# Order of the four query blocks within a group of two attention loops: narrow, wide, middle narrow, middle wide

## The reference, cut to what matters

```python
# first loop: nsa_attention, the selected and the window branch
s = jnp.einsum('bgmqd,bgqkld->bgmqkl', qb, ks)           # selected keys
o_sel = jnp.einsum('bgmqkl,bgqkld->bgmqd', softmax(s, tok <= tq), vs)
s = jnp.einsum('bgmqd,bgsd->bgmqs', qb, kwb)             # window keys
o_win = jnp.einsum('bgmqs,bgsd->bgmqd', masked_softmax(s, win_ok), vwb)

# second loop: dilated attention (8 heads) and forgetting attention (8 heads)
s = jnp.einsum('bqhd,bkhd->bhqk', qi, k) * SCALE          # + bias or decay
s = jnp.where(k_pos[None, :] <= q_pos[:, None], s, NEG_INF_2)
o = jnp.einsum('bhqk,bkhd->bqhd', jax.nn.softmax(s, axis=-1), v)
```

## Time and profile before

| | us |
|---|---|
| median of 3 runs (1836.47 to 1839.16) | 1838.65 |
| span of the profiled execution | 1837.4 |
| first loop in it, first scores to the end | 98.2 |
| second loop in it, first scores to the end | 82.0 |

### The profile page before, as it was taken

The page is one execution under the profiler, slowest core; times in us unless marked ns, Lnnn a source line. Parts: engine busy times, 40 slices in busy tenths (PEclk is TensorE's granted clock), DMA queues, the critical chain, the costliest instruction groups (busy, mean ns, idle before and its releaser), DMA issues. The chain is left out here.

```text
span 1837.4 us, 22565 instructions
## 1 busy us (share of the span) xinstructions
PE 1760.4 (96%) x9024; PEld 1289.9 (70%) x9024; DVE 858.7 (47%) x1672; ACT 627.8 (34%) x1248; POOL 235.1 (13%) x286
## 2 busy tenths in 40 slices
PE   7999999999999999999999999999999989999993
PEld 6778888888888787568888888888766663333330
DVE  4436544543367345745554453263347562333224
ACT  5236344323353224635433332253347320000001
POOL 4000000000001003310000000000014404333322
PEclk9999999999999998999999999999999999999997
DMA  7223333332232217303333322332320158999974
GB/s 236 90 76 84 100 91 91 97 109 92 92 121 92 69 65 228 111 25 91 92 95 109 93 92 92 104 127 91 93 92 24 55 228 330 376 398 389 380 311 151
DMA packets 179528, 261.02 MB, mean 142 GB/s; under 512 B 18904, under 2 KB 134824, under 8 KB 167152
## 3 DMA queue, kind: packets, MB, share of 16 engines
q1 hardware_dynamic: 155824, 204.66, 33.2%
q0 software_dynamic: 19584, 25.77, 4.4%
q10 hardware_dynamic: 4032, 29.36, 4.1%
HBM read 297.53 MB, written 29.40 MB: 178 GB/s over the span
## 5 line engine op out<-in xcount | busy, mean ns | idle before, releaser
L189 PE MATMUL PB<-RING_R,OPS_R 128*128 128x512 f32 (+1 forms) x1056 | 414.7, 393 | 5.1 <-DVE RING_R L152 4.1
L191 PE MATMUL PB<-RING_R,OPS_R 128*128 128x512 f32 (+1 forms) x1056 | 409.1, 387 | 0.0
L190 PE MATMUL PB<-RING_R,OPS_R 128*128 128x512 f32 (+1 forms) x1056 | 408.9, 387 | 0.0
L169 DVE SCALAR_TENSOR_TENSOR RING_R<-RING,gains,RING_R 128x256 fp32r<-128x256 f32 (+2 forms) x456 | 219.4, 551 | 253.8 <-ACT RING_R L167 253.8
L189 PE MATMUL PB<-OPS_R,RING_R 128*128 128x512 f32 (+1 forms) x736 | 280.7, 381 | 0.0
L190 PE MATMUL PB<-OPS_R,RING_R 128*128 128x512 f32 (+1 forms) x736 | 279.5, 380 | 0.0
L191 PE MATMUL PB<-OPS_R,RING_R 128*128 128x512 f32 (+1 forms) x736 | 279.5, 380 | 0.0
L189 PEld LDWEIGHTS PB<-RING_R,OPS_R 128*128 128x128 f32 x1056 | 198.8, 188 | 48.4 <-DVE RING_R L152 5.3
L167 ACT ACTIVATE RING_R<-RING,gains 128x256 fp32r<-128x256 f32 (+2 forms) x456 | 209.9, 541 | 59.2 <-DMA RING<-in_w_in 47.7
L191 PEld LDWEIGHTS PB<-RING_R,OPS_R 128*128 128x128 f32 x1056 | 198.8, 188 | 40.7
L190 PEld LDWEIGHTS PB<-RING_R,OPS_R 128*128 128x128 f32 x1056 | 199.0, 188 | 38.9 <-issue 0.2
(11 more groups left out here) (379 smaller groups left out, 2033.1 us busy)
## 6 DMA issues: line engine op xcount, KB each, us to landing
RING<-in_ffn_w_gate SPq DMA_DIRECT2D x44, 512.0 KB, 4.0
RING<-in_ffn_w_up SPq DMA_DIRECT2D x44, 512.0 KB, 5.2
RING<-in_ffn_w_down SPq DMA_DIRECT2D x44, 512.0 KB, 4.2
RING<-in_w_expert_gate SPq DMA_DIRECT2D x16, 1024.0 KB, 8.0
RING<-in_w_expert_up SPq DMA_DIRECT2D x16, 1024.0 KB, 11.6
OPS<-in_w_expert_gate SPq DMA_DIRECT2D x16, 1024.0 KB, 13.6
OPS<-in_w_expert_up SPq DMA_DIRECT2D x16, 1024.0 KB, 16.2
Y<-in_w_expert_down ACTq DMA_DIRECT2D x14, 1024.0 KB, 9.6
```

Source lines behind the costliest of these rows:

```text
L169: t = nc.vector.scalar_tensor_tensor(by_k(RING_R, o)[:, :, k, :], raw, g, high.bitcast(fp32), ALU.mult, ALU.subtract)
L189: nc.tensor.matmul(o, x[0], w[0], start=start, stop=False)
L190: nc.tensor.matmul(o, x[0], w[1], start=False, stop=False)
L191: return nc.tensor.matmul(o, x[1], w[0], start=False, stop=stop)
```

## The change

The units are the same; the list order differs. In the first loop the branch r is now outside the block i, so that both runs over the four blocks follow one another; in both loops the blocks come in the order 0, 3, 1, 2, in widths w1 w4 w2 w3. Two conditions in values() of the second loop, which stood for "first unit of a group" and "last unit of a group", are rewritten so that they still mean that. All waits on semaphores count units, not widths, and the counts are made by functions that go by the width of each unit, so they follow.

```diff
@@ -1511,7 +1511,8 @@
-        NSA = [(c, i, r) for c in range(4) for i in range(MT) for r in range(2)]
+        BY_WIDTH = (0, 3, 1, 2)
+        NSA = [(c, i, r) for c in range(4) for r in range(2) for i in BY_WIDTH]
@@ -1913,7 +1914,7 @@
-        TWO = [(f, c, i) for f in range(2) for c in range(4) for i in range(MT)]
+        TWO = [(f, c, i) for f in range(2) for c in range(4) for i in BY_WIDTH]
@@ -1995,7 +1996,7 @@
-                if i == 0 and n >= 2:
+                if u % MT == 0 and n >= 2:
@@ -2007,7 +2008,7 @@
-                if i == MT - 1:
+                if u % MT == MT - 1:
```

## The result

The kernel with the new order takes 1842.3 us (median of 20 runs, 1837.8 to 1850.7), the kernel before on the same chips 1838.6 (20 runs, 1836.5 to 1843.1). The ratio is 1.0022, 95% interval 1.0013 to 1.0031: slower by 3.7 us. The forecast was 1838.3 and no change. The profiled execution has a span of 1839.9 us, before 1837.4.

The account below looks back on a forecast made before the run. It took chains through several engines to bound the two loops, PE being busy 96% of the span. First loop -0.4 and second +0.1 made -0.3 us, so 1838.65 became 1838.3, no change; range 1834.3 to 1842.5.

Parts of the forecast that it names:

- sum of distances: Both loops: times between successive values steps on PE, added per group; 9.28 us for the new order against 9.41.
- the paragraph on PE's clock: Low level only from 711.5 to 725.5, costing 0.40 us per us; upper level for the rest of the first loop.
- turn 15 is a w3: First loop: DVE's maxima and 2.3 us split precede the w3 copy; 4.2 instead of 2.24, so 2.0 us more.
- With the release where it is: Assumes the first loop's 14 us low-clock stretch ends as before, leaving the forecast sum at -0.3 us.
- the clock stays low longer: Rival, first loop's start: release 14 us later costs 5.6 us, giving 1843.9; chance 4%.
- A clock row below 1.00 behind 730: Sign in the first loop's clock that would prove the rival of a longer low clock, 1843.9 us.
- The clock rises sooner: Rival, first loop's start: a shorter low stretch saves 4 us, giving 1834.3; chance 7%.
- DVE late for the wide copies: Rival, both loops: late maxima delay the w3 copy, 16 x 0.33 = 5.3 us, giving 1843.6; chance 8%.
- Scores hidden: Rival: every distance a copy chain, a group 8.62 instead of 9.28, 10.6 us less, 1827.7; chance 4%.
- scores chain: Distance set by PE's values, transposes and scores in order; for w2 behind w4 2.69 us, against copy chain 2.31.

Follow-up runs that it names:

- e1: Changed kernel with the new order in the first loop alone, the second loop keeping rising width; 1841.9 us, ratio 1.0015 to the kernel before.
- e6: Changed kernel with no weight split inside the first loop, both chunks split behind it; 1840.5 us, ratio 1.0002 to the kernel before.
- e3: Changed kernel with the first loop's weight splits one turn later (ACT in turns 15, 23; DVE in 16, 24); 1831.0 us, ratio 0.9955 to the kernel before.
- e5: Kernel before (old order) with the first loop's weight splits one turn later; 1839.0 us, ratio 1.0001 to the kernel before.
- e9: Changed kernel with DVE's part of each first-loop split in halves, in turns 16 and 18 (24 and 26); 1831.3 us, ratio 0.9958 to the kernel before.
- e4: Kernel before (old order) with two unread DVE reductions behind each first-loop weight split; 1843.7 us, ratio 1.0026 to the kernel before.
- e10: New order with splits one turn later, plus two unread DVE reductions ahead of the w3 copies of turns 15 and 23; 1840.0 us, ratio 1.0007 to the kernel before.
- e7: Changed kernel with DVE's part of each first-loop split in halves, in turns 15 and 17 (23 and 25); 1834.8 us, ratio 0.9976 to the kernel before.

## Why the prediction was wrong

**The sum of distances was right.** The first loop by its four groups, from the values of turns 7, 15, 23 and 31, in us:

| first loop | before | after | moved | forecast | same list, upper level |
|---|---|---|---|---|---|
| first scores to turn 7 | 32.01 | 29.17 | -2.8 | -0.4 | |
| to turn 15 | 22.94 | 23.47 | +0.5 | +0.6 | |
| to turn 23 | 21.94 | 26.73 | +4.8 | +0.7 | +0.6 (e1, 22.52) |
| to turn 31 | 20.25 | 21.97 | +1.7 | -1.1 | -1.0 (e6, 19.26, no split) |
| last values | 1.02 | 0.80 | -0.2 | -0.2 | |

Where the clock is up, each group is within about 0.1 us of the forecast. The second loop confirms it: a group with f = 0 is 9.29 (forecast 9.28), with f = 1 9.71 (1401.05 to 1410.76; forecast 9.74), the two with sums and split 21.45 (21.7), the fourth values 12.4 behind the first scores (12.6). In all it moved by -0.3, forecast +0.1.

**The step that failed is the paragraph on PE's clock.** It read the earlier trace rows rightly, one low stretch at the start, and then treated its release as all that could move: everything behind it was taken at the upper level, "for the rest". The same text had worked out the cause of the new falls: "turn 15 is a w3 ... 4.2 instead of 2.24". It priced that as 2.0 us of wait and went on. It had the earlier trace rows beside it, a fall right behind a wait of 1.23, and didn't ask whether a wait of 2.2 that the change makes could do the same. It does: behind 757 and 784 the profile has 10.2 + 6.8 = 17.1 us of low clock, and by 0.4 each they are 6.8 us, which is the +4.2 and the +2.7 by which the third and fourth group exceed the same list at the upper level.

The same paragraph was wrong a second time, the other way: "With the release where it is" the first stretch was left at its 14 us, and it became 6.8. The first group moved by -2.8 where -0.4 was forecast, a figure given without its working.

Two of the rivals also leaned on the wait of the earlier trace rows staying as it was ("the same wait of PE stands in the same place", "PE's wait for ACT stays"). It doesn't: with the new list PE waits 0.60 in place of 1.23 us there, and the clock falls all the same (at 709.56), as PE's timeline of after shows:

```profile
705.50 3.76 PE L1619 MATMUL PB<-kcT,ST 64*128 64x32 f32 x64
709.87 1.23 PE L1555 MATMUL PB<-STG,ST 64*128 64x256 f32 x4 [0.60 <-ACT Z L1652]
```

All twelve profiles have a fall at this place, between 708.8 and 712.1, behind the third branch's 64 small matmuls. So the length of the wait alone doesn't decide; the work before it may count too, which no run separates.

**The rival that came nearest** was "the clock stays low longer". It had the kind, the price and its sign (it ended at 1843.9), but it was placed at the first release, and its chance of 4% was worked out for that place. A clock row below 1.00 behind 730 was named as what would prove it; there are two, though the first release came sooner, not later. "The clock rises sooner" came true in that place: the first low stretch is 6.8 us instead of 13.7, which by 0.4 is 2.7 of the first group's 2.8. Over the profiles it holds: the first low stretch is 10 to 17 us in the three others with the old list in the first loop, and 3 to 7, once 10, in the eight with the new one. "DVE late for the wide copies" didn't come: in the second loop's group above no wait stands in front of the w3 values. Only where the split stands in front is a w3 copy late, by 2.2 us. "Scores hidden" fell as argued: 2.67 for w2 behind w4 is a scores chain.

**Why +3.7 and not +7.** The falls cost 6.9 us in the profiled execution, but the first group gives back 2.4 more than its forecast. The first loop is 4.0 longer and the second 0.3 shorter, 3.6 together by unrounded times, and this execution (1841.9 us) lies near the median. Nor do the falls come in every execution. After's 20 timed runs go from 1837.8 us with a mean clock of 0.988 to 1850.65 with 0.981, and the shortest, at before's own clock (0.988), is 0.5 us from the forecast. Over all 20 the times follow the clock: a straight line through them has 1.4 us for each 0.001, which is 3.7 us at the lower level, so 0.38 us for each, near the 0.41 above. In the mean over the runs the clock is 0.9849, in the kernel before 0.9876 to 0.9880 (its runs beside the experiments): 5.0 to 5.7 us of full clock, 10 to 11 us at half, by 0.4 an estimated 4.0 to 4.6 us, against 3.7 measured. The wide spread of after is the same thing seen from outside.

**Where e3's gain comes from.** Its profile is 6.8 us shorter than before's: the first loop -5.7, of which the shorter low stretch at its start (6.8 instead of 13.7 us) would be some 2.7, and the three later groups 2.7 (1.5, 0.9 and 0.3); the second loop -0.3; the remaining 0.8 lies outside the loops, where nothing was changed (-1.8 ahead of them, +1.0 behind), and is not explained, though behind them a low stretch of 6.8 us in e3 (from 1508.1) stands for one of 3.4 in before (from 1517.1). The share of the order's own DVE slack and of fewer occasional falls in the timed runs (mean clock 0.9900) was not separated.

**What stays open.** Why the same wait of 2.19 lowers the clock in one place of e1's profile and not in the other was not settled. Nor why, with the old order in the second loop, e1 and e5 fall there behind a wait of 1.00 us (e5 at 1430.1, for 3.4 us), where before, with the same wait, does not; nor why e1, e5 and e9 fall for 3.4 us near that loop's start, and the others don't.

The Trainium skill (TensorE: Matmul & The Clock Gate, Part 1: The HAM clock gate) says that activity releases the throttle and idleness brings it back. The trace agrees in kind: each of the two new falls of after's first loop stands behind a wait of 2.19 us in which PE was idle. The prediction drew on that rule for the release alone, not for a wait of its own making.

## What to carry to other kernels

Price a new order together with the work that hangs at fixed places of the old one: list every such piece and ask in front of whose copy it now lies. A forecast wait of some 2 us on PE is two terms: its length, and what the clock may cost behind it, in this kernel's loop about 0.4 us for each us at the lower level. A wider spread of the timed runs is the sign to look for it in the windows, and since one profile shows one execution, the mean clocks of the timed runs belong beside it. When a change disappoints by its hung-in work, move that work to the place that the new order covers before dropping the order.

## What the runs showed of the hardware

Of the eight waits between 1.97 and 2.19 us that PE had inside the first loop (two each in after, e1, e4 and e10), seven had a fall to the lower level between their end and 1.6 us later. It lasted 3.4 to 10.2 us, though PE was busy nearly all through it. In e7's profile there was none behind its waits of 1.12 us in the same turns, and none in e3's behind its longest wait in that loop, 0.87. At other places shorter waits did have a fall in them or behind them: 1.00 in the second loop of e1 and e5, and 0.60 or 1.23 at the first loop's start in every profile. So the length of a wait gives no rule by itself. After e6's wait of 4.81 us, in which the clock fell, back-to-back matmuls took 0.63 us in place of 0.39 for 5.6 us (801.64 to 807.3), one every 0.43 us instead of every 0.23.
